# FFN-down matmuls taken pass by pass over eight PSUM banks instead of bank by bank

## The reference

```python
def conv_ffn(h, w_up, conv_w, conv_b, w_down):
    up = h @ w_up                                   # 512x1024 @ 1024x5632
    upc = lax.conv_general_dilated(up, conv_w, ...) + conv_b   # width 3, per channel
    gate, val = upc[..., :D_FF], upc[..., D_FF:]    # D_FF = 2816
    return (jax.nn.silu(gate) * val) @ w_down       # 512x2816 @ 2816x1024
```

## Time and profile before

| | us |
|---|---|
| median of 3 runs | 774.94 (774.71, 774.94, 779.1) |
| the profiled execution, own time | 775.91 |
| its span in the profile | 774.1 |
| PE busy | 726.4 (94%) |
| DVE busy | 433.9 (56%) |
| ACT busy | 302.2 (39%) |
| mean DMA rate | 96 GB/s |

### The profile page before, as it was taken

How to read it: one execution, slowest core, us unless ns; L and a number is a source line. 1 busy time by engine, 2 the same in 40 slices (tenths; PEclk the granted TensorE clock), 3 DMA queues, 4 the chain that set the end, 5 groups by cost and what they waited for, 6 DMA issues and landing times.

```text
span 774.1 us, 10474 instructions
## 1 busy us (share of the span) xinstructions
PE 726.4 (94%) x3737; PEld 601.9 (78%) x3737; DVE 433.9 (56%) x734; ACT 302.2 (39%) x501; POOL 126.1 (16%) x145
## 2 busy tenths in 40 slices
PE   3897886998899999999999999999999999999998
PEld 3686775886677778878789888888888887888886
DVE  4571995792476644576776755555556474333332
ACT  5561412332567533353444533343433343232320
POOL 0999944400312000011001000000000000000000
PEclk9899878986999999999999999999999999999999
DMA  9339214244351300330303332233322332223302
GB/s 261 115 118 156 70 29 124 43 160 141 96 191 55 108 1 1 137 109 1 109 1 110 109 108 89 74 108 108 108 65 97 108 108 97 71 105 108 108 0 110
DMA packets 62855, 73.94 MB, mean 96 GB/s; under 512 B 20729, under 2 KB 46628, under 8 KB 62692
## 3 DMA queue, kind: packets, MB, share of 16 engines
q1 hardware_dynamic: 58580, 73.19, 30.9%
q10 hardware_dynamic: 4240, 0.28, 0.5%
HBM read 68.08 MB, written 5.78 MB: 95 GB/s over the span
## 4 chain that ended last, share of the span: by engine, by line
PE 77%; DVE 11%; DMA 3%; ACT 3%; issue 3%; SPq 2%; ACTq 1%; POOL 0%; DVEq 0%
PE pb L489 22%; PE pb L491 21%; PE pb L490 21%; PE pb L1606 9%; DVE F L1113 4%; PE pb L1609 3%; DMA raw<-in_w_in 2%; DVE wring L472 1%; DMA scr_y<-F 1%; ACT L785 1%; ACT F L785 1%; DVE wring L475 1%; SPq L577 1%; ACTq L809 1%; DVE xs L1119 1%
## 5 line engine op out<-in xcount | busy, mean ns | idle before, releaser
L472 DVE TENSOR_TENSOR wring<-raw,wring 128x1024 fp32r<-128x1024 f32 x100 | 125.7, 1259 | 114.5 <-ACT wring L461 114.2
L489 PE MATMUL pb<-xs,wring 128*128 128x512 f32 (+1 forms) x432 | 164.4, 381 | 7.0 <-DVE wring L472 6.8
L491 PE MATMUL pb<-xs,wring 128*128 128x512 f32 (+1 forms) x432 | 163.1, 377 | 0.0
L490 PE MATMUL pb<-xs,wring 128*128 128x512 f32 (+1 forms) x432 | 163.0, 377 | 0.0
L461 ACT ACTIVATE wring<-raw 128x1024 fp32r<-128x1024 f32 x100 | 104.7, 1052 | 120.8 <-PE pb L491 102.7
L1119 DVE SCALAR_TENSOR_TENSOR F<-pb,ccol,F 128x511 f32<-128x511 f32 x88 | 65.9, 749 | 103.4 <-ACT F L785 97.5
L1606 PE MATMUL pb<-F 128*128 128x64 f32 (+6 forms) x736 | 90.8, 314 | 14.2 <-DVE F L1281 8.3
L489 PEld LDWEIGHTS pb<-xs,wring 128*128 128x128 f32 x432 | 82.4, 191 | 23.0 <-DVE wring L472 7.7
L489 PE MATMUL pb<-wring,bs 128*128 128x512 f32 x240 | 97.7, 407 | 0.9 <-DVE F L1119 0.5
L491 PE MATMUL pb<-wring,bs 128*128 128x512 f32 x240 | 94.2, 392 | 0.0
L490 PEld LDWEIGHTS pb<-xs,wring 128*128 128x128 f32 x432 | 82.5, 191 | 14.8
(11 more groups left out here) (128 smaller groups left out, 761.2 us busy)
## 6 DMA issues: line engine op xcount, KB each, us to landing
raw<-in_ffn_w_up SPq DMA_DIRECT2D x22, 1024.0 KB, 5.1
raw<-in_ffn_w_down SPq DMA_DIRECT2D x11, 1024.0 KB, 4.9
raw<-in_w_in SPq DMA_DIRECT2D x8, 1024.0 KB, 7.9
F<-in_x SPq DMA_DIRECT2D x8, 512.0 KB, 5.1
raw<-in_x_wkv SPq DMA_DIRECT2D x4, 1024.0 KB, 5.1
raw<-in_w_out SPq DMA_DIRECT2D x4, 1024.0 KB, 4.9
raw<-in_x_wq SPq DMA_DIRECT2D x2, 1024.0 KB, 6.3
raw<-in_x_wo SPq DMA_DIRECT2D x2, 1024.0 KB, 5.8
```

What stands on the lines that cost most here:

```text
L472: ins = nc.vector.tensor_tensor(w_unit(u, 1), raw_unit(u), w_unit(u, 0).bitcast(f32), ALU.subtract)
L489: nc.tensor.matmul(ps, lh, rh, start=first, stop=False)
L490: nc.tensor.matmul(ps, lh, rl_, start=False, stop=False)
L491: return nc.tensor.matmul(ps, ll, rh, start=False, stop=last)
```

## The change

In `down_unit`, the three products are the outer loop and the eight banks the inner one: first high x high for banks 0 to 7, then high x low for banks 0 to 7, then low x high for banks 0 to 7. Each bank still gets its three matmuls of a unit, in the same order among themselves, with the same operands; between two of them there are now seven of the other banks. The wait of `fill` stands ahead of a bank's first matmul in unit 0, as before, and the raise of `unit_used` is on the last of the 24 matmuls, as before. The last three units, and all other engines, are as they were.

```diff
                 pe.wait_ge(act_lo, r * 4 + (n + 1))
-                for b in range(8):
-                    t, half = b // 2, b % 2
-                    p = fill(pe, f"d{b}") if n == 0 else pb[b]
-                    at = slice(n % 4 * 512 + t * 128, n % 4 * 512 + (t + 1) * 128)
-                    cols = slice(half * 512, (half + 1) * 512)
-                    last = mm3(p[:, :], bs[:, 0, at], bs[:, 1, at], w_unit(u, 0)[:, 0, cols], w_unit(u, 1)[:, 0, cols],
-                               n == 0, False)
+                for i, (a_part, w_part) in enumerate(((0, 0), (0, 1), (1, 0))):
+                    for b in range(8):
+                        t, half = b // 2, b % 2
+                        p = fill(pe, f"d{b}") if n == 0 and i == 0 else pb[b]
+                        at = slice(n % 4 * 512 + t * 128, n % 4 * 512 + (t + 1) * 128)
+                        cols = slice(half * 512, (half + 1) * 512)
+                        last = nc.tensor.matmul(p[:, :], bs[:, a_part, at], w_unit(u, w_part)[:, 0, cols],
+                                                start=n == 0 and i == 0, stop=False)
                 last.then_inc(unit_used, 1)
```

## The result

| | before | changed |
|---|---|---|
| median of 18 runs each, us | 774.67 (773.04 to 779.1) | 776.38 (774.98 to 780.52) |
| ratio, with 95% interval | | 1.0036 [1.0021, 1.0051] |
| profiled execution, own time / span, us | 775.91 / 774.1 | 775.99 / 774.2 |

The medians differ by 1.71 us; the forecast was 776.3 us and 1.36 us more. The change is slower by a fifth to half of a per cent, which this many runs tell apart from zero, and within the 1% that counted as no change. Wherever a ratio is given, two executions of the kernel before at 1189 and 1426 us, far above all others, are left out of it.

The account below looks back on a forecast made before the run. PE was taken to set the pace; the longer wait for bank 3 added 1.36 us and all other terms nothing, so 774.94 + 1.36 = 776.3 us. The range was 774.6 to 778.5 us.

Parts of the forecast that it names:

- What bounds it: FFN down: PE sets the pace, with one 0.5 us wait from 649 us to the end.
- The wait for bank 3, +1.36 us: Unit 0 of FFN down: bank 3 becomes fourth matmul instead of tenth, release unchanged; 1.99 us lost instead of 0.63.
- The pace, 0 between -6.1 and +0.4 us: Units 0 to 18: changing bank at every matmul costs nothing, taken as 0.
- The slower rival: All 456 changed matmuls: changing bank each time upsets the pace, giving about 826 us; chance 0.04.
- the faster one: Changed units: no neighbours in the same bank saves 6.1 us, giving 770.2 us; chance 0.06.
- The low bound: Pace term, units 0 to 18: all 456 matmuls save a fixed 13.3 ns each, 6.1 us.
- The other banks, and who waits for a unit: nothing: FFN down: the other seven banks are free before use, and later splits keep 13 us of cover; no cost.
- The clock in the longer wait, 0.13: Rival after unit 0's wait for bank 3: the clock falls, 1.4 us more, 777.7 us; chance 0.13.
- The size: Whole kernel: median 776.3 us, 1.36 us more, 0.2% slower; within 1% with chance 0.95.

Follow-up runs that it names:

- without the wait: Kernel before, still bank by bank, but with banks 4 to 7 first: stretch 119.68 us in both traces, ratios 0.9975 and 0.9981.
- The run without a wait: Changed kernel with unit 0 bank by bank, banks 4 to 7 first: stretch 119.67 us, ratio to the kernel before 0.9978.
- two of 2.60: Changed kernel with bank 3 first in every pass, traced twice: stretches 122.57 and 122.54 us, ratio 1.004 to the kernel before.
- three of three with 3.12 or 3.89: Changed kernel with DVE freeing bank 3 later, in its own order (124.68 us stretch) and with bank 3 first (125.45 and 125.42 us).

## Why the prediction was right

**What bounds it.** Right. PE was the bound throughout, and every microsecond taken from it or given to it in unit 0 came out at the end: the stretch was 1.37 us longer in the changed kernel and 0.77 us shorter without the wait.

**The wait for bank 3, +1.36 us.** Right, and measured four ways: 1.37 in the changed kernel, 1.36 with unit 0 alone changed, 1.35 in the second trace of the change, and 0.02 with unit 0 alone undone. That DVE would release the bank at the same distance from f43, and that the idle time in brackets would read 1.8 us, held as well. The absolute times of the forecast (653.02 and 771.9 us) did not hold, since the stage began 1.30 us earlier; they should have been given as distances from the last FFN-up matmul.

**The pace, 0 between -6.1 and +0.4 us.** Right at 0. The run without a wait confirms for 24 changes of bank in 24 matmuls what the two stages before the change had told for fewer. The slower rival and the faster one fall together: no spread of accumulation over banks gave or cost anything that can be read. The spacing stayed at 81.66 / 360 = 226.8 ns. From its first to its last matmul, the changed kernel's FFN down had the granted clock at 1.00, and PE was idle once in it.

What the Trainium skill ("TensorE: Matmul & The Clock Gate", section "A second HAM failure mode: psum-queue depth-cycling") reports of a kernel that cycled through banks with frequent short idle times, a clock that swings between its two levels, was thus not seen here. The same page's section "Back-to-back issue gap" has 215.8 ns for a spacing by its formula, which it gives for an isolated matmul; the measured 226.8 ns decides.

The bounds of this term were worked out loosely. The low bound lets all 24 matmuls of a unit save 13.3 ns, though in the old order only 16 of them followed one to the same bank: 19 x 16 x 13.3 ns is 4.0 us and not 6.1. FFN up has seven more such neighbours in 24 matmuls than FFN down, not eight, so 0.09 us a unit and not 0.11. Neither changes the choice of 0.

**The other banks, and who waits for a unit: nothing.** Right; PE had no second wait in any trace. One premise was off without effect: PE still issued transposes for the residual rows, into banks 4 to 7, in the first tiles of FFN up, at 413.69 and 417.45 us. That is over 230 us ahead of FFN down.

**The clock in the longer wait, 0.13.** Right to give it the smaller chance. It did not fall in three traces with a wait of 1.8 us in brackets nor in two of 2.60, and fell in three of three with 3.12 or 3.89. Eight traces don't show that the length of the wait alone decides.

**The size.** Right in the trace, with an open end in the timed runs. Medians differ by 1.71 us and the ratio of 1.0036 stands for 2.8 us, with 1.6 as its lower end, more than the 1.37 us of the stretch. That the forecast of 776.3 us met the measured 776.38 so closely is partly luck: the base of the forecast, a median of 3 runs, was 0.27 us above the median of 18, and the timed step was 0.35 us larger than forecast.

Part of the surplus is an uneven share of long executions. The changed kernel had five of 18 runs above 779 us and the one before one of 18 in that comparison. None of the five was traced. Their mean granted clock was 0.954 to 0.958, as in the seven of 35 long runs of the kernel before (0.954 to 0.956), where the other runs of the changed kernel had 0.960 to 0.968. With the four traces of such executions this makes it likely that their extra time lies ahead of FFN down; for the five it is argued and not shown.

The other part stays open. Without these long runs the means still differ by 2.03 us. The medians also moved further than the stretch, and the same way, in all eight timed comparisons in which the stretch changed: 1.71 for 1.37, 1.83 for 1.36, 0.58 for 0.45, 3.06 for 2.12 and 5.33 for 5.00 us longer; 1.71 and 1.24 for 0.77 and 1.57 for 0.78 us shorter. No trace shows where that comes from: ahead of FFN down the traces differ by up to 2.2 us whatever the kernel, even without the long ones.

## What to carry to other kernels

When an order of matmuls over several accumulators changes, look first at when each accumulator is first touched: the bank that was freed last should come last; here the work for the free banks went ahead of it at no cost (119.68 against 120.45 us). Interleaving products over the banks neither helped nor hurt an engine that already ran without gaps (119.67 against 119.68 us). Compare the changed stretch between two fixed instructions, since one span can hide a loss of 1.4 us behind an earlier start.

## What was not expected of the hardware

The same idle time ended in both ways. Ahead of a transpose PE waits 1.42 us, up to 203.56 us in the kernel before and up to 203.95 in the trace of unit 0 alone by pass. In the first the pace stays. In the second, PE's timeline reads:

```profile
203.95 0.33 PE L1609 MATMUL pb<-ident,F 128*128 128x128 f32 x1 [1.42 <-ACT F L785]
...
206.18 0.63 PE L490 MATMUL pb<-wring,bs 128*128 128x512 f32 x1
206.61 0.63 PE L491 MATMUL pb<-wring,bs 128*128 128x512 f32 x1
```

The starts are 0.43 us apart, the level of 1.2 GHz. Together with the longer low stretch near 260 us this makes that execution 3.35 us late at FFN down. The three other long executions have the same 1.42 us of idle there, and the same 0.43 us between starts after it. So an idle time with small matmuls behind it may be followed by the lower level in one execution and not in the next, while waits of up to 2.60 us among dense 512-column matmuls left the clock alone in all five traces.
